# A differential-attention stage with filler and convolution taps dealt out over its parts by another plan

## The reference

```python
p = softmax(q1 @ k1.T * scale + bias) - lam * softmax(q2 @ k2.T * scale + bias)   # causal, per head
a = p @ v                                                        # 8 heads, q and k of 64, v of 128
a = rms_norm(a, subln_w) * (1 - lam_init)
u_a, u_b = split(u)
c = causal_depthwise_conv(u_a * sigmoid(u_b), conv_w, conv_b)    # 31 taps, 1,024 channels
g = sigmoid(g + gate_b)                                          # gates, 2,048 columns
```

## Time and profile before

| what | value |
|---|---|
| time before, median of 3 runs | 3486.72 us (3485.94 to 3488.28) |
| the profiled execution, its own time | 3477.37 us |
| its span, first to last instruction | 3475.5 us |
| PE busy | 2984.8 us, 86% |
| DVE busy | 1583.8 us, 46% |
| ACT busy | 1231.7 us, 35% |
| POOL busy | 710.7 us, 20% |
| stage changed | 1,287 to 2,254 us of the span |

### The profile page before, as it was taken

The page is one execution under the profiler, slowest core; times in us unless marked ns, Lnnn a source line. Parts: engine busy times, 40 slices in busy tenths (PEclk is TensorE's granted clock), DMA queues, the critical chain, the costliest instruction groups (busy, mean ns, idle before and its releaser), DMA issues. The chain is left out here.

```text
span 3475.5 us, 35301 instructions
## 1 busy us (share of the span) xinstructions
PE 2984.8 (86%) x13448; PEld 2411.8 (69%) x13448; DVE 1583.8 (46%) x1931; ACT 1231.7 (35%) x2003; POOL 710.7 (20%) x317
## 2 busy tenths in 40 slices
PE   6999998767769949898988989785886998998998
PEld 5787886656657737676776777663675887787786
DVE  3665651356654135877787777513322110121121
ACT  3555541334431144555555545423213111111110
POOL 2111111100002112322333223212222112121111
PEclk8999999878879969999999999988897999999999
DMA  4111222122213212112121112142320111111112
GB/s 108 43 47 57 59 75 61 22 56 45 48 55 121 97 70 61 55 50 63 38 63 55 57 50 76 64 151 91 121 109 25 42 42 49 43 48 42 43 42 73
DMA packets 239268, 218.87 MB, mean 63 GB/s; under 512 B 29304, under 2 KB 200856, under 8 KB 239128
## 3 DMA queue, kind: packets, MB, share of 16 engines
q1 hardware_dynamic: 238096, 215.41, 20.4%
q10 hardware_dynamic: 1032, 1.57, 0.3%
HBM read 156.66 MB, written 41.42 MB: 57 GB/s over the span
## 5 line engine op out<-in xcount | busy, mean ns | idle before, releaser
L179 POOL TENSOR_TENSOR w_lo<-w_raw,w_hi 128x1024 fp32r<-128x1024 f32 (+3 forms) x228 | 535.8, 2351 | 2167.5 <-ACT w_hi L171 2167.5
L171 ACT ACTIVATE w_hi<-w_raw 128x1024 fp32r<-128x1024 f32 (+3 forms) x228 | 224.0, 985 | 787.6 <-PE u_y_ps L1763 222.8
L2386 DVE SCALAR_TENSOR_TENSOR d_acc<-d_padded,vectors,d_acc 128x1024 f32<-128x1024 f32 x240 | 396.5, 1652 | 4.5
L197 PE MATMUL d_pp<-h_hi,w_hi 128*128 128x512 f32 x896 | 367.2, 410 | 12.2 <-PEq L67 5.2
L197 PE MATMUL d_pp<-h_hi,w_lo 128*128 128x512 f32 x896 | 367.8, 411 | 0.0
L197 PE MATMUL d_pp<-h_lo,w_hi 128*128 128x512 f32 x896 | 364.7, 407 | 0.0
L197 PE MATMUL s_pp<-h_hi,w_hi 128*128 128x512 f32 x512 | 206.1, 403 | 12.2 <-PEq L67 12.2
L197 PEld LDWEIGHTS d_pp<-h_hi,w_hi 128*128 128x128 f32 x896 | 174.3, 195 | 56.2 <-issue 18.1
L2170 POOL TENSOR_TENSOR d_probs<-d_probs 128x128 f32<-128x128 f32 (+3 forms) x64 | 123.7, 1933 | 406.6 <-ACT d_probs L2284 406.6
L197 PE MATMUL s_pp<-h_hi,w_lo 128*128 128x512 f32 x512 | 204.8, 400 | 0.0
L197 PE MATMUL s_pp<-h_lo,w_hi 128*128 128x512 f32 x512 | 203.7, 398 | 0.0
(11 more groups left out here) (333 smaller groups left out, 6545.6 us busy)
## 6 DMA issues: line engine op xcount, KB each, us to landing
w_raw<-in_w_in SPq DMA_DIRECT2D x97, 512.0 KB, 4.0
w_raw<-in_w_gate_up SPq DMA_DIRECT2D x44, 512.0 KB, 3.9
w_raw<-in_w_down SPq DMA_DIRECT2D x22, 512.0 KB, 3.7
gates<-s_gate SPq DMA_DIRECT2D x16, 512.0 KB, 5.3
f_gate<-gates SPq DMA_DIRECT2D x16, 512.0 KB, 5.2
w_raw<-in_w_out SPq DMA_DIRECT2D x16, 512.0 KB, 3.7
w_raw<-in_w_proj SPq DMA_DIRECT2D x16, 512.0 KB, 4.9
x_tok_in<-in_x SPq DMA_DIRECT2D x8, 512.0 KB, 7.9
```

The lines of the kernel that those rows point to most:

```text
L171: act.activation(self.hi[:, s, 0:chunks, :], self.raw[:, s, 0:chunks, :], ACT.Copy).then_inc(self.rounded[s], 1)
L179: pool.tensor_tensor(self.lo[:, s, 0:chunks, :], self.raw[:, s, 0:chunks, :], f32(self.hi[:, s, 0:chunks, :]), ALU.subtract).then_inc(self ...
L197: mm = pe.matmul(halves(ps)[h], w[:, k, :], x[:, k, h * HALF:(h + 1) * HALF], start=(k == 0 and r == 0), stop=(k == chunks - 1 and r == 2))
L2386: dve.scalar_tensor_tensor(out=acc[:, :], in0=x, scalar=wt, in1=acc[:, :], op0=ALU.mult, op1=ALU.add).then_inc(c["taps"], 1)
```

## The change

The filler of a head is dealt so that the filler and the fixed work of PE (`pe_work`) fill every part to one level. That gives for head 2, in matmuls per part: b0 16 14 15, b1 15 0 9, b2 13 9 16, b3 6 12 16, b4 12 15 16, b5 11 8 16, b6 10 14 16, b7 9 5 15. Taps are dealt the same way against `dve_work`: b0 2 2 2, b1 1 1 2, b2 0 2 2, b3 0 1 2, b4 1 - -, b5 - 2 2, b6 1 2 2, b7 0 2 2. At x = 0 the odd tap runs in the part's first half. `values` moves from x = 0 to x = 1; the first chunk's turns, `round_t` and `low_t` from x = 0 to x = 1 (the second chunk's stay at x = 2). ACT's square of k runs behind the `take` of its part. Taps may go on one part longer.

```diff
-        weight = [13, 13, 13, 13, 12, 12, 11, 11]
+        V_TURN, Q_SQUARE, O_SQUARE, K_SQUARE = 4, 5, 6, 8
+        def pe_work(h, at):
+            b, x = divmod(at, PARTS)
+            turned = min(4, b) if b else 4
+            work = {V_TURN: 0.9, Q_SQUARE: 1.7 * (h < LAST), O_SQUARE + 1: 1.7 * (h > 0),
+                    K_SQUARE + 1: 1.7 * (h < LAST)}.get(at, 0)
+            if x == 0:
+                work += 0.23 * (b + 1)
+            if x == 1:
+                work += 0.11 * turned + {1: 2.9, 3: 0.7, 5: 1.5, 7: 2.2}.get(b, 0)
+            if x == 2:
+                work += 0.11 * (max(b - 4, 0) if b else 4)
+            return work
...
-            at = [base + total * sum(weight[:b]) // sum(weight) for b in range(QB + 1)]
-            ends += [[lo + (hi - lo) * x // PARTS for x in range(PARTS + 1)] for lo, hi in zip(at, at[1:])]
+            fixed = [pe_work(h, at) for at in range(PARTS * QB)]
+            room = 0.231 * each[h] * SIX
+            for lower in sorted(fixed):
+                under = [f for f in fixed if f <= lower]
+                if sum(lower - f for f in under) <= room:
+                    level = (room + sum(under)) / len(under)
+            total, share = 0.0, [max(level - f, 0) for f in fixed]
...
-        conv_end = [part_of[stream.index(("a", h)), 0] - 2 for h in range(1, HEADS)] + [PARTS * (STEPS - 1)]
+        conv_end = [part_of[stream.index(("a", h)), 0] - 1 for h in range(1, HEADS)] + [PARTS * (STEPS - 1) + 1]
-        TAP = 1.45
+        TAP = 1.65
...
-            share = (other + TAP * n) / time
-                upto = n if at == room[-1] else min(n, max(done, int((share * t - o) / TAP)))
+            level = (sum(dve_work(at) for at in room) + TAP * n) / len(room)
+            free = [max(level - dve_work(at), 0.2) for at in room]
+                upto = n if at == room[-1] else round(n * total / sum(free))
...
-                    if h < LAST and at == K_SQUARE:
-                        square_of("k", h + 1)
                     if s < STEPS:
                         for t, e in halves_in(s, x):
                             if stream[t][0] != "a":
                                 take(t, e)
...
+                    if h < LAST and at == K_SQUARE:
+                        square_of("k", h + 1)
                     u = s - 1
-                    if x in (0, 2) and 0 <= u < STEPS and x // 2 < CHUNKS[u % QB]:
-                        round_t(u, x // 2)
+                    if x > 0 and 0 <= u < STEPS and x - 1 < CHUNKS[u % QB]:
+                        round_t(u, x - 1)
...
-                    for t in range(x + (y - x) * lo // 4, x + (y - x) * hi // 4):
+                    middle = x + (y - x + (at % PARTS == 0)) // 2
+                    for t in range(x, middle) if first_half else range(middle, y):
                         tap(h, t)
...
-                    if x in (0, 2) and 0 <= u < STEPS and x // 2 < CHUNKS[u % QB]:
-                        low_t(u, x // 2)
+                    if x > 0 and 0 <= u < STEPS and x - 1 < CHUNKS[u % QB]:
+                        low_t(u, x - 1)
...
-                    if x == 0 and s >= 3 and s % 2 == 1:
+                    if x == 1 and s >= 3 and s % 2 == 1:
                         values((s - 3) // 2)
                     u = s - 1
-                    if x in (0, 2) and 0 <= u < STEPS and x // 2 < CHUNKS[u % QB]:
-                        turn_t(u, x // 2)
+                    if x > 0 and 0 <= u < STEPS and x - 1 < CHUNKS[u % QB]:
+                        turn_t(u, x - 1)
```

More of the change, by code:

```diff
@@ L2021, in differential_and_conv @@
         TILES = len(stream)
-        weight = [13, 13, 13, 13, 12, 12, 11, 11]
+        V_TURN, Q_SQUARE, O_SQUARE, K_SQUARE = 4, 5, 6, 8
[11 more added lines that the diff above has]
+            return work
         ends, base = [], 0
         for h in range(HEADS):
-            total = each[h] * SIX
-            at = [base + total * sum(weight[:b]) // sum(weight) for b in range(QB + 1)]
-            base += total
-            ends += [[lo + (hi - lo) * x // PARTS for x in range(PARTS + 1)] for lo, hi in zip(at, at[1:])]
+            fixed = [pe_work(h, at) for at in range(PARTS * QB)]
+            room = 0.231 * each[h] * SIX
+            level = 0.0
+            for lower in sorted(fixed):
[3 more added lines that the diff above has]
+            total, share = 0.0, [max(level - f, 0) for f in fixed]
+            at = [base]
+            for x in share:
+                total += x
+                at.append(base + round(each[h] * SIX * total / sum(share)))
+            base += each[h] * SIX
+            ends += [at[PARTS * b:PARTS * (b + 1) + 1] for b in range(QB)]
         def part(s, x):
@@ L2050, in differential_and_conv, with dve_work @@
         conv_in_at = [-1] + [part_of[stream.index(("a", h)), 1] for h in range(1, HEADS)]
-        conv_end = [part_of[stream.index(("a", h)), 0] - 2 for h in range(1, HEADS)] + [PARTS * (STEPS - 1)]
+        conv_end = [part_of[stream.index(("a", h)), 0] - 1 for h in range(1, HEADS)] + [PARTS * (STEPS - 1) + 1]
         TAPS_FIRST = 13
-        TAP = 1.45
-        def pe_load(at):
+        TAP = 1.65
+        def dve_work(at):
             s, x = divmod(at, PARTS)
[L2058 to L2067, removed]
-            load += sum(0.7 for t, e in halves_in(s, x) if stream[t][0] == "a")
-            return load + (1.7 + 0.27 * (b + 1) + 0.4 if x == 0 else 0.5 if x == 2 and b > 4 else 0)
-        V_TURN, Q_SQUARE, O_SQUARE, K_SQUARE = 4, 5, 6, 8
+            h, b = divmod(s, QB)
+            load = {V_TURN: 1.4, Q_SQUARE: 1.3, Q_SQUARE + 1: 2.7, O_SQUARE + 1: 1.3, K_SQUARE + 1: 1.3,
+                    K_SQUARE + 2: 2.5}.get(at % (PARTS * QB), 0) * (h < LAST or at % (PARTS * QB) in (V_TURN, O_SQUARE + 1))
+            load += sum(0.7 for t, e in halves_in(s, x) if stream[t][0] == "a")
+            if x == 0:
+                load += 0.5 + (1.15 + 0.28 * (b + 1) if b < 4 else 0.8 + 0.285 * (b + 1))
+            if x == 1:
+                load += 0.15 + 0.135 * (min(4, b) if b else 4)
+            if x == 2 and (b == 0 or b > 4):
+                load += 0.15 + 0.135 * (b - 4 if b else 4)
+            return load
         taps_in = {}
@@ L2075, in differential_and_conv @@
             n = CONV - (TAPS_FIRST if h == 0 else 0)
-            time, other = [sum(f(at) for at in room) for f in (pe_load, dve_load)]
-            share = (other + TAP * n) / time
-            done, t, o = 0, 0.0, 0.0
-            for at in room:
-                t, o = t + pe_load(at), o + dve_load(at)
-                upto = n if at == room[-1] else min(n, max(done, int((share * t - o) / TAP)))
+            level = (sum(dve_work(at) for at in room) + TAP * n) / len(room)
+            free = [max(level - dve_work(at), 0.2) for at in room]
+            total, done = 0.0, 0
+            for at, x in zip(room, free):
+                total += x
+                upto = n if at == room[-1] else round(n * total / sum(free))
                 taps_in[at] = (h, CONV - n + done, CONV - n + upto)
@@ L2387, in tap, with taps @@
                                              op1=ALU.add).then_inc(c["taps"], 1)
-            def taps(at, lo, hi):
+            def taps(at, first_half):
                 if at in taps_in:
                     h, x, y = taps_in[at]
-                    for t in range(x + (y - x) * lo // 4, x + (y - x) * hi // 4):
+                    middle = x + (y - x + (at % PARTS == 0)) // 2
+                    for t in range(x, middle) if first_half else range(middle, y):
                         tap(h, t)
@@ L2492, in _ @@
                     at = b * PARTS + x
-                    taps(PARTS * s + x, 0, 2)
+                    taps(PARTS * s + x, True)
                     if s < STEPS and x == 0:
@@ L2514, in _ @@
                         low_k(h + 1)
-                    taps(PARTS * s + x, 2, 4)
+                    taps(PARTS * s + x, False)
             normalise("o", LAST)
```

## The result

The changed kernel takes 3513.78 us (median; 3511.51 to 3517.12), the kernel before 3486.33 beside it: ratio 1.0082, interval 1.0066 to 1.0098. It is slower by 27.5 us. The forecast was 3501, in the range 3455 to 3523; the direction is right, the time is inside the range, and the size is half of what came. The profiled executions differ by more, 3509.7 against 3475.5 us of span: the one of before reached the stage 3.1 us earlier (1287.5 against 1290.6) and spent 2.4 us less behind it. The stage itself, from its first matmul to the first of the next stage, lasts 988.0 us before and 1016.7 after: +28.7.

What follows compares the result with a forecast made beforehand. The DVE-ACT loop was taken to bound heads 0 to 5, PE heads 6 and 7. Head terms -2.5 + 3 x 4 - 1 - 3 + 8 + 1 = +14.5 us on 3486.7 gave 3501 us, range 3455 to 3523.

Steps and rivals of the forecast that it cites:

- The signs named ahead: Profile after: taps about 1.5 us, line 341 wait gone, 7 us DVE wait at line 2472, 11 us PE waits for `feed_conv`.
- The waits of heads 1 to 4: DVE's waits, mostly on ACT, change by +8.1 to 31.5 us a head.
- the sigmoid's `low_t`: Part 13's `low_t`, heads 1 to 4: DVE waits 7.0 us behind ACT's sigmoid run, before none; bounds 5.4 to 7.5.
- the 4 in the forecast: Net added time per head in heads 1 to 4, taken between +4.6 and +3.0, giving 114.3 us.
- The contention: DVE taps beside POOL: cost falls from 10.5 to 7 us a head, a gain of 3.5; bounds 10.5 and 4.
- The 0.45 us for each microsecond of POOL: Price of POOL running beside a DVE tap, taken from four taps of 2.3 us each doing the work of 1.285.
- Head 6: PE-bound; an 11 us PE wait for `feed_conv` at tile v, then 60 us of PE work: +8 us.
- Head 7: Gate tiles alone, PE-bound; second chunks' turns cost 0 to 3 us: +1 us.
- Head 5: DVE's clumps of taps come apart: about 118.5 us instead of 121.67, -3 us.
- A: Rival, parts 20 to 24 and 9 to 13: PE's stalls go and DVE follows, faster, 3451 us; chance 0.29.
- B: Rival: the moves cancel, new DVE waits near 27 us a head, same time, 3487 us; chance 0.21.
- C: Rival: contention stays 10.5, turns' stalls make PE the bound with slow clock, 4 more us in 5 heads, 3520; chance 0.12.

Runs made afterwards that it cites:

- the turns back: Changed kernel with values, first turns, `round_t` and `low_t` back at x = 0 as before: 3499.8 us, +13.7 against the kernel before.
- e4_border: Changed kernel with the border repair: three matmuls moved from part 12 to part 11 in heads 1 to 6; 3500.4 us, +14.1 against the kernel before.
- e8_values_alone: Kernel before with only the values' product moved from x = 0 to x = 1: 3519.8 us, +33.8, ratio 1.0092.
- the repairs and the taps ahead: Changed kernel with border moved, turns and values as before, second half of taps ahead of `normalise`: 3465.8 us, 0.9946 of before.

## Why the prediction was right, and what it missed

The signs named ahead came: PE's 7.1 us wait at line 341 is gone, a DVE wait of 6.7 us stands right behind ACT's second table load, PE waits 10.7 and 9.4 us for `feed_conv` in heads 5 and 6, and the mean tap is 1566 ns for the "about 1.5 us" of the sign. The time lies 0.8 us above my forecast's own range, 3490 to 3513, and not for the reason that this range was made for: heads 1 to 3 did what was foretold, heads 6 and 7 did not.

**The waits of heads 1 to 4: the places right, the sum in part by luck.** 114.3 us were foretold for a head, 114.2 came. Item by item, foretold and measured in head 2: the sigmoid's `low_t` 7.0 and 6.73; `low_q` 3.1 and 2.96; `normalise` of k 3.7 and 3.64, of q 1.2 and 1.20; `low_k` 0.7 and 0.66; `weights` of steps 4, 6 and 7 0.55, 0.9, 2.5 and 0.54, 0.96, 2.37; `low_t` of steps 6 and 7 3.0, 1.6 and 2.76, 1.55. Step 5's 1.0 did not come, and step 1 gave 1.7 instead of 2.45: the sum grew by 5.2 us, not by 8.1. Against that, DVE's busy time fell by 1.7 and not by 3.5. The two misses, 2.9 and 1.8 us, point opposite ways and mostly cancel, and the 4 in the forecast was chosen between two sums, 4.6 and 3.0. That 114.2 came so near is luck on top of a right account. Of PE's waits in such a head, about 6 us at the start of tile v came (5.9); the 5 for step 4's exponentials did not, and the second chunks' turns of steps 6 and 7 gave 3.1 and 0.7. The changed kernel's sigmoid starts 1.30 us after the beginning of the load before it too (1651.42 and 1652.72 above). By the Trainium skill, "ScalarE: Activation LUTs", section What ACT_TABLE_LOAD costs, a switch of table has a drain of about 1.38 us beyond the load. It is not to be seen here either: the load takes 1.28 us and the sigmoid starts 0.02 us after its end.

**The contention: the place right, the price misread.** The prediction read the four taps of the earlier trace rows as "2.3 each". That is a mean of two kinds. One by one, beside POOL's mix and weight subtraction, in the kernel before:

```profile
1679.97 1.28 DVE L2386 SCALAR_TENSOR_TENSOR d_acc<-d_padded,vectors,d_acc 128x1024 f32<-128x1024 f32 x1
1680.17 3.33 POOL L2170 TENSOR_TENSOR d_probs<-d_probs 128x1024 f32<-128x1024 f32 x1 [6.16 <-ACT d_probs L2284]
1681.29 3.29 DVE L2386 SCALAR_TENSOR_TENSOR d_acc<-d_padded,vectors,d_acc 128x1024 f32<-128x1024 f32 x1
1683.46 3.32 POOL L179 TENSOR_TENSOR w_lo<-w_raw,w_hi 128x1024 fp32r<-128x1024 f32 x1
1684.62 3.25 DVE L2386 SCALAR_TENSOR_TENSOR d_acc<-d_padded,vectors,d_acc 128x1024 f32<-128x1024 f32 x1
```

The first tap, begun before the mix, takes its 1.28 us; the fourth, at 1687.90 and alone, 1.29. The two between end 1.08 us after the POOL instruction that was running when they began. This holds in the whole stage: 183 of the 240 taps of before take 1.3 to 1.4 us, and the other 57, of 1.6 to 3.3 us, all end 1.08 or 1.09 us after such an instruction. So a tap isn't slowed evenly. It comes out as if it had stood until POOL was done, and its price is what was left of POOL's instruction when it began. The mix takes 3.33 us here, where a tap was running when it began, and 2.37 in the changed kernel, where none was. The 0.45 us for each microsecond of POOL was an average over one clump.

Counted in head 2, POOL and taps run at the same time for 19.9 us before and 12.3 after (23 and 15 to 16 in the prediction), and the taps take 10.4 and 8.0 us more than their 1.285 each (10.5 and 7). So the taps gained 2.4 us and not 3.5, and the multiplication that opens a tile's taps now meets a subtraction and gives 1.7 of them back:

```profile
1663.84 2.88 DVE L2406 TENSOR_SCALAR d_acc<-d_padded,vectors 128x1024 f32<-128x1024 f32 x1
```

It took 1.21 us before.

The cause was to be taps dealt apart. With the taps alone the mean stays at 1655 ns; with the turns alone it is 1593, in the change 1566, and with the turns back 1657. The overlap says why: over the stage mix and taps run together for 80 us before, 74 with the taps alone, 38 with the turns alone, 31 in the change and 71 with the turns back. The moved turns take the mix out of the taps. The subtraction is the other half (78 us before, 74 in the change), and it explains the two runs that don't fit the turns alone: e4_border has 32 us of mix but 94 of subtraction beside taps, and 1624 ns; e8_values_alone 76 and 69, and 1614.

**Head 6: a term that was mis-sized.** +8 was foretold, +12.7 came. The wait was as foretold: PE stands 9.4 us for `feed_conv` (11 foretold; 10.7 in head 5).

```profile
PE d_pp L197 <- DVE d_padded L2431: 9.4, 1, 9.4
```

By the marks of the prediction: the scores of step 5 come at 50.2 us behind the maximum of step 2 (48 foretold, 38.7 before), and the next head's maximum 63.3 us behind them, for which the prediction had 60 of work and 1 of waits. The same stretch took 62.2 before, so half of what was missed there stood in the trace of before. The other miss is ahead of step 5: PE came back at 42.3 us, as foretold, but took 7.9 us to the scores and not 6. The clock had gone down during the wait, and PE came out of it at the lower level:

```profile
2114.80:2120.10 5.30, 0.00 (x0) 0.01 (x1) 3.38 (x6) 2.34 (x5) 0.00 (x0) 0.50 0.24 99
2120.10:2125.00 4.90, 4.88 (x14) 3.92 (x15) 1.70 (x3) 2.68 (x5) 3.89 (x2) 0.50 0.00 0
```

The granted clock is 0.50 there, 1.2 of 2.4 GHz, and 1.00 on both sides. For half of that time PE had nothing to do, so the low clock costs at most half of 4.9 us, 2.5. The border repair checks it. In the same head it has the same 479 matmuls at 1.00:

```profile
2072.82:2180.91 108.09, 99.63 (x479) 79.75 (x478) 71.21 (x84) 58.19 (x100) 32.03 (x15) 1.00 0.23 70
```

PE is busy 99.6 us and not 101.2, 1.5 less, and waits 8.5 and not 12.4. So of the 12.7 us some 8.4 are waits (4.0 before), 1.5 the clock, and the rest, by difference 2.8, goes with 12 more matmuls in the window than before. A mean clock over a head overstates what it costs when the clock is low while PE stands: 0.95 of 113.6 us would be 5.7. The prediction had counted the clock as a gain and nowhere as a loss.

**Head 7: the term that was mis-sized most.** +1 was foretold, +5.8 to step 7 came and about 1.4 behind it. The second chunks' turns were priced at 0 to 3 us. PE waited 2.0 and 3.0 us for `low_t` in steps 5 and 6 and 2.4 in step 7, and the clock was 0.97, not 1.00 (0.5 for 3.4 us of full work, 1.7 us by estimate). The turns moved alone cost this head 3.9 us, and with the turns back 1.8 are left, so they are most of it.

**Head 5: a gain that the wait ate.** -3 was foretold from DVE's clumps coming apart, -0.4 measured. With the border repaired, which takes 6.7 us off the wait for `feed_conv`, head 5 takes 118.6, the 118.5 of the forecast. So the gain is there and the forecast had put the wait at nothing for this head. That the clumps held it was not tested by itself.

Head by head, foretold and measured: -2.5 and -2.6 up to head 1; +12 and +11.8 in heads 1 to 3; -1 and 0; -3 and -0.4; +8 and +12.7; +1 and +7.2. The sum is 14.5 and 28.7. Of the 14 us missed, 11 are in the two heads that PE bounds.

**The rivals.** A (PE's stalls go and DVE follows) fell: the 7.1 us wait did go, and the head got longer. It comes in part with the repairs and the taps ahead. B fell: the new waits were 28.6 us, near its 27, but the kernel is slower beyond noise. C's 3520 is nearer to what came than my 3501, and part of its mechanism came: the turns' stalls and the slow clock, but in heads 6 and 7 and not as 4 us in each of five heads, and the contention did fall.

## What to carry to other kernels

When a plan deals work evenly over slots, look at what ends at the slots' borders: here three matmuls on the wrong side of one cost 13 us, since the jobs that wait for the tile's end (a table switch and a sigmoid, the convolution's input) moved to a place where nothing was left to cover them. Follow a wait to what its releaser itself waited for before saying which engine sets the period. And an order that one buffer's reuse imposes (product, then turns) is part of the price of each edit taken alone: the values' product alone gave +34 us, with the turns +27. Plans that are cut for each other have no price alone either: the filler gave +50, the taps +12, the turns +27, and the whole 27.5.

## What was not expected of the hardware

A wait of PE can cost twice, and the second price depends on where the lower clock falls. In head 6 the run of the taps alone had 5.9 us of waits, a clock of 0.95 and some 4 us of slower matmuls. The changed kernel had 12.4 us of waits and the same 0.95, and only 1.5 us of slower matmuls, since PE stood still for half of the low stretch.

A DVE tap and a POOL addition or subtraction that meet don't share. Each of the 57 long taps before ends 1.08 us (one 1.09) after the POOL instruction that it met, and so do the 50 of the changed kernel (1.08 or 1.09), as if it had stood until then. A tap takes 1.28 us alone and up to 3.3, and the mix of 1024 columns 2.37 when no tap is running as it begins and 3.33 when one is. The same 64 mixes took 1933 ns on average before (1980 in head 2) and 1542 after, the same 240 taps 1652 and 1566, with only their order changed.
